# Ten units of the first block as seven products of block sums instead of eight block products

## The chip, the cores and the metric

The kernel runs on one core of a Trainium2 chip. The metric is the device time of one execution in microseconds. The engines named below are TensorE (PE: matmul; PEld: its weight loads), VectorE (DVE), ScalarE (ACT), GpSimd (POOL) and SyncE (SP, which here only starts DMAs). They run side by side and wait for each other by semaphores. Each executes its own instructions in their written order.

## What is computed

Two blocks follow each other on 512 tokens of 1024 channels; the change lies in the first. Its reference, cut to what matters:

```python
h = rmsnorm(x, norm_g[l])
proj = jnp.einsum('bsd,dn->bsn', h, w_in[l])            # 1024 -> 12 x 1024
a_u, a_v, a_z, b_p, b_z, c_h, c_b, c_c, c_z, gate_logits = jnp.split(proj, SPLIT_OFFSETS, axis=-1)
ya = spatial_gating(gelu(a_u), gelu(a_v), ...) * silu(a_z)
yb = multiscale_pool(b_p, ...) * silu(b_z)
yc = c_b * causal_depthwise_conv(c_c * c_h, conv_w[l], conv_b[l]) * silu(c_z)
gates = sigmoid(gate_logits.reshape(bsz, s, 3, 1024))   # g0, g1, g2
merged = gates[:, :, 0] * (ya @ w_branch_a) + gates[:, :, 1] * (yb @ w_branch_b) + gates[:, :, 2] * (yc @ w_branch_c)
x = x + merged @ w_out
```

Everything is float32. Each float32 matrix is used as two parts that TensorE takes: a high part (rounded) and a low part (the rest). A product is three matmuls: high x high, high x low, low x high.

## The kernel before

A section is one 1024 x 1024 weight matrix applied to all 512 tokens; it has two units of 512 output channels (c_h.0, c_h.1). The list `JOBS` (L70 and after) names all jobs in the order in which TensorE does them: ..., b_z, pool.0, pool.1, g1, c_h, w_b, c_c, g2, c_b, c_z, w_c, w_out, and so on. It also holds how often a job's semaphores are raised, from which `chunks_before`, `used_after`, `act_after` and `dve_after` work out every wait.

A unit has four chunks of 256 input channels x 512 outputs, 512 KB each. SP loads a chunk into one of four slots of `WR` (`RING` = 4) as soon as VectorE has made the low part of the chunk that was there before. ScalarE copies it to `WH` (high part, `split`, L999) once TensorE is through with the chunk that used the slot; VectorE writes `WL` = `WR` - `WH` (`split`, L1570); TensorE waits for that (`low_ready`) and does 24 matmuls per chunk: two groups of 128 input channels, four banks of 128 outputs, three high and low combinations, each over 512 token columns (`unit`, L2471). A unit is 96 such matmuls and fills the four banks of its parity; the next unit has the other four. The tokens' high and low parts are `HH` and `HL` (from `h`) or `YH` and `YL` (from a branch).

The banks are then emptied: the g units by ScalarE with a sigmoid into `G` and c_h by ScalarE into `CH` (`evac`, L1037); c_c and c_b by VectorE, multiplied as they leave the bank (L1850, L1871), with the three taps of the convolution in between (L1855, L1861); c_z by ScalarE with silu through `TMP`. `merge` (L1829, L1831) multiplies a branch's product by its gate and adds it to `M`.

Around pool.1, VectorE multiplies the pooled branch into `CH` (L1811, L1816), ScalarE makes its high parts `YH` and VectorE its low parts `YL` (`y_low`, L1607), and then the four chunks of g1.1 are split. GpSimd computes tables in the first 126 us has two copies and two small memsets up to 232 us, and nothing more until after c_z. The second copy of the input, `X`, is loaded behind the chunks of c_h.

## Time and profile before

| | |
|---|---|
| time, median of 3 runs | 1618.98 us (1618.83 to 1619.22) |
| span of the profiled execution | 1617.1 us |
| busy: TensorE, weight loads | 1606.0 us (99%), 1344.3 us (83%) |
| busy: VectorE, ScalarE, GpSimd | 952.0 us (59%), 667.2 us (41%), 204.3 us (13%) |
| instructions | 19917 |

The span is the time from the first to the last instruction of one execution that was profiled; the runs' time has some 2 us more around it. A busy share is an average over stages, so what a stage is bound by is read from its waits and from the chain that ended last, which follows from the last instruction back to what released each. Matmuls overlap at their ends: two starts in a row show the pace, a single duration doesn't.

### The profile page before, as it was taken

To read this page: it belongs to the slowest core of one execution; us is meant where nothing else is said; L and a number is where in the kernel's file an instruction comes from. 1 tells how busy PE (TensorE), PEld (TensorE's weight loads), DVE (VectorE), ACT (ScalarE), POOL (GpSimd) and SP (SyncE) were. 2 spreads that over 40 slices of the span, in tenths; PEclk is the share of its full clock that TensorE was granted. 3 is DMA by queue.
4 is the path that set the end of the run, shared out by engine and by line. 5 is a ranking of instruction groups with operands and counts; after the bars stand their busy time and mean duration, and the time that the engine had idled before them with its cause. 6 is when DMAs were issued, how large, how long until landed. Compare 5 with 4: busy or idle time off the path is not lost.

```text
span 1617.1 us, 19917 instructions
## 1 busy us (share of the span) xinstructions
PE 1606.0 (99%) x7833; PEld 1344.3 (83%) x7833; DVE 952.0 (59%) x1325; ACT 667.2 (41%) x936; POOL 204.3 (13%) x237
## 2 busy tenths in 40 slices
PE   9999999999999999999999999999999999999998
PEld 7888888888888888888898889887888888888887
DVE  5267274663235424456899999985473535455357
ACT  5333342253222223335455454558255425343254
...
GB/s 243 172 171 135 164 118 93 76 93 103 157 96 98 95 103 92 102 93 80 314 166 204 189 194 220 105 205 182 194 72 93 66 90 106 54 77 91 79 77 66
DMA packets 152395, 207.41 MB, mean 128 GB/s; under 512 B 52289, under 2 KB 75509, under 8 KB 151670
## 3 DMA queue, kind: packets, MB, share of 16 engines
...
HBM read 191.53 MB, written 14.68 MB: 128 GB/s over the span
## 4 chain that ended last, share of the span: by engine, by line
PE 97%; DVE 1%; ACT 1%; DMA 0%; issue 0%; DVEq 0%; SPq 0%; ACTq 0%
PE PS L2471 82%; PE PS L2449 3%; PE PS L2839 1%; PE PS L2548 1%; PE PS L2789 1%; PE PS L2691 1%; PE PS L2869 1%; PE PS L2658 1%; PE PS L2641 0%; PE PS L2845 0%; PE PS L2717 0%; PE PS L2626 0%; PE PS L2715 0%; PE PS L2716 0%; ACT XN L1006 0%; PE PS L2826 0%
## 5 line engine op out<-in xcount | busy, mean ns | idle before, releaser
L2471 PE MATMUL PS<-HH,WH 128*128 128x512 f32 x1216 | 474.7, 390 | 0.8 <-ACT G L1037 0.4
L2471 PE MATMUL PS<-HH,WL 128*128 128x512 f32 x1216 | 473.3, 389 | 0.0
L2471 PE MATMUL PS<-HL,WH 128*128 128x512 f32 x1216 | 473.2, 389 | 0.0
L999 ACT ACTIVATE WH<-WR 128x1024 fp32r<-128x1024 f32 x200 | 211.9, 1061 | 596.9 <-PE PS L2471 558.9
L1570 DVE TENSOR_TENSOR WL<-WR,WH 128x1024 fp32r<-128x1024 f32 x144 | 186.1, 1299 | 391.9 <-ACT WH L999 391.3
L2471 PEld LDWEIGHTS PS<-HH,WH 128*128 128x128 f32 x1216 | 228.3, 188 | 49.4 <-issue 2.1
L2471 PEld LDWEIGHTS PS<-HH,WL 128*128 128x128 f32 x1216 | 228.3, 188 | 47.8
L2471 PEld LDWEIGHTS PS<-HL,WH 128*128 128x128 f32 x1216 | 228.3, 188 | 47.0
L2022 DVE SCALAR_TENSOR_TENSOR TMP<-CP,PRM,TMP 128x512 f32<-128x512 f32 x232 | 155.0, 748 | 0.0
L2471 PE MATMUL PS<-WH,HH 128*128 128x512 f32 x320 | 126.8, 396 | 0.0
L2471 PE MATMUL PS<-WL,HH 128*128 128x512 f32 x320 | 125.1, 391 | 0.0
L2471 PE MATMUL PS<-WH,HL 128*128 128x512 f32 x320 | 125.1, 391 | 0.0
L2471 PE MATMUL PS<-YH,WH 128*128 128x512 f32 x320 | 124.6, 389 | 0.0
L2471 PE MATMUL PS<-YH,WL 128*128 128x512 f32 x320 | 124.5, 389 | 0.0
L2471 PE MATMUL PS<-YL,WH 128*128 128x512 f32 x320 | 124.5, 389 | 0.0
L1601 DVE TENSOR_TENSOR WL<-WR,WH 128x1024 fp32r<-128x1024 f32 x64 | 76.3, 1220 | 52.5 <-ACT WH L1025 52.5
L1025 ACT ACTIVATE WH<-WR 128x1024 fp32r<-128x1024 f32 x64 | 66.3, 1058 | 83.0 <-PE PS L2471 81.8
L2471 PEld LDWEIGHTS PS<-WH,HH 128*128 128x128 f32 x320 | 67.9, 212 | 13.1 <-issue 3.0
L2471 PEld LDWEIGHTS PS<-WH,HL 128*128 128x128 f32 x320 | 67.9, 212 | 10.5 <-issue 0.7
L2471 PEld LDWEIGHTS PS<-WL,HH 128*128 128x128 f32 x320 | 67.9, 212 | 10.1
L2471 PEld LDWEIGHTS PS<-YL,WH 128*128 128x128 f32 x320 | 60.1, 188 | 12.5
L2471 PEld LDWEIGHTS PS<-YH,WH 128*128 128x128 f32 x320 | 60.1, 188 | 12.5
...
## 6 DMA issues: line engine op xcount, KB each, us to landing
WR<-in_w_in_dram SPq DMA_DIRECT2D x96, 512.0 KB, 3.8
WR<-in_od_w_in_dram SPq DMA_DIRECT2D x32, 512.0 KB, 4.0
WR<-in_ev_w_in_dram SPq DMA_DIRECT2D x24, 512.0 KB, 4.6
WL<-in_ev_w_in_dram POOLq DMA_DIRECT2D x24, 512.0 KB, 7.6
WR<-in_ev_w_in_dram SPq DMA_DIRECT2D x32, 256.0 KB, 3.1
WR<-in_ev_w_out_dram SPq DMA_DIRECT2D x16, 512.0 KB, 5.3
WR<-in_od_w_in_dram SPq DMA_DIRECT2D x32, 256.0 KB, 3.4
WR<-in_od_w_out_dram SPq DMA_DIRECT2D x16, 512.0 KB, 3.8
```

The source lines that it names most:

```text
L999: act.activation(WH[:, n % RING, :, :], WR[:, n % RING, :, :], ACT.Copy).then_inc(w_hi, 1)
L1025: act.activation(WH[:, j % RING, :, :], WR[:, j % RING, :, :], ACT.Copy).then_inc(w_hi, 1)
L1570: dve.tensor_tensor(WL[:, s, :, :], WR[:, s, :, :], WH[:, s, :, :].bitcast(F32), ALU.subtract).then_inc(w_lo, SUM_TO - SUM_FROM + 1 if n = ...
L1601: dve.tensor_tensor(WL[:, s, :, :], WR[:, s, :, :], WH[:, s, :, :].bitcast(F32), ALU.subtract).then_inc(w_lo, 1)
L2022: o = dve.scalar_tensor_tensor(CP[:, kt, CPAD:] if last else TMP[:, s, :], CP[:, kt, k:k + SEQ], w, TMP[:, s, :], ALU.mult, ALU.add)
L2449: mm = pe.matmul(out_banks[m], tok(acts(kt)[ai], m), (WH, WL)[wi][:, q, kk, :], start=(kt == 0 and i == 0), stop=(kt == KT - 1 and i == 2))
L2471: mm = pe.matmul(out_banks[m], st, mv, start=(kt == 0 and i == 0), stop=(kt == 2 * per - 1 and i == 2))
L2548: mm = pe.matmul(bank("a_v.0", t), tile(H(2 * q + kk)[ai], t), (WH, WL)[wi][:, q, kk, :], start=(q == 0 and kk == 0 and i == 0), stop=(q = ...
L2658: mm = pe.matmul(bank(f"pool.{i}", m), (PWH, PWL)[wi][:, g, k, (kt % 2) * P:(kt % 2 + 1) * P], Y(2 * g + k)[ai], start=(k == 0 and j == 0) ...
L2691: mm = pe.matmul(bank(f"s5_z.{i}", m)[:, r * P:(r + 1) * P], WT[m // 2][:, pr, :], UT[:, pr, :], start=True, stop=True)
L2789: mm = pe.matmul(out_bank[:, cols], tile(acts(kt)[ai], t), (WH, WL)[wi][:, 2 * u + kt // 2, kt % 2, cols], start=(kt == 0 and i == 0), sto ...
L2839: mm = pe.matmul(A[m][:, s * P:SEQ], (V2, V2L)[wi][:, s, m * P:(m + 1) * P], scores, start=(s == 0 and i == 0), stop=(s == TT - 1 and i == ...
```

## The change

The ten units of c_h, c_c, g2, c_b and c_z become products of 2 x 2 blocks: halves of the tokens (256), of the input channels (512) and of the unit's outputs (256). Eight block products would be the same work as before; here seven products of sums of blocks are made, and their sums give the four output blocks.

- Each product is 24 matmuls of 256 columns (four groups of input channels, two of outputs, three high and low combinations). The seven operands of a unit are split like chunks, each of the same size as before (128 x 1024), in the four slots of `WH` and `WL`.
- SP loads the four weight blocks of a unit into places 0 to 3 of the `WR` region (rows of 1 KB instead of 2 KB). GpSimd adds blocks in place: W0 += W1, W1 += W2, W0 += W2, W3 += W0. The operands are, in order: block 0, sum 1, sum 2, sum 3, block 3, block 2, sum 4. A place is loaded again for the next unit when its last operand is split; place 0 when the fourth sum is made.
- The sums of token blocks are made once. When pool.1 is done, GpSimd does ten additions or subtractions of 128 x 1024 (from `HH` and `HL`); ScalarE and VectorE split the four results into high and low parts. The fourth replaces a block of `HH` and `HL`, once g1.1 is done.
- Products go to banks 0, 1, 3, 2 and then again 0, 1, 3, without clearing for the last three. ScalarE copies bank 0 out after product 0 and again after product 4. VectorE makes five combinations of a bank with a block already in SBUF; product 5 waits for the second, product 6 for the third, since they read the banks that these products go on with.
- In VectorE's queue these five stand between the low parts of the own and of the following unit. The side work (taps, products with c_b and c_z, low parts of Y) is dealt out between them as `others`, up to eight operations per unit, from c_c.1 on. It now reads SBUF only, since the combined units lie there. The sigmoid of g2 and the silu of c_z are done in place behind the combinations.
- The load of `X` moves behind c_z.1. Four semaphores of the tables become one.

The core of the diff:

```diff
-_section("c_h", a=4)
+_seven("c_h", (0, 2))
 _section("w_b", d=4)
-_section("c_c", d=4)
-_section("g2", a=4)
-_section("c_b", d=4)
-_section("c_z", a=4)
+_seven("c_c")
+_seven("g2")
+_seven("c_b")
+_seven("c_z")
...
+BLOCK_AT = ((0, 0), (0, 1), (1, 1), (1, 0))
+OPERAND_AT = (0, 0, 1, 0, 3, 2, 3)
+OPERAND_SUM = {1: 1, 2: 2, 3: 3, 6: 4}
...
+                for place in (1, 0, 2, 3) if again else range(4):
+                    if again and place == 0:
+                        sp.wait_ge(sums_made, sums_after(j - 1))
+                    elif again:
+                        sp.wait_ge(w_lo, chunks_before(before) + (0, 3, 6, 7)[place])
+                    else:
+                        sp.wait_ge(w_lo, n0 - RING + place + 1)
+                    i, half = BLOCK_AT[place]
+                    c0 = W_IN[name] + int(u) * NC + half * (NC // 2)
+                    sp.dma_start(WRS[:, place, :, :], w_in[4 * P * i:4 * P * (i + 1), c0:c0 + NC // 2]
+                                 .rearrange("(k p) n -> p k n", p=P)).then_inc(w_loaded[place], 16)
...
+            pool.wait_ge(side_done, side_after("pool.1"))
+            tt(S1R[:, :, :], h_part(HH, 1, 1), h_part(HH, 1, 0), ALU.subtract)
+            tt(STMP[:, :, :], h_part(HL, 1, 1), h_part(HL, 1, 0), ALU.subtract)
+            seq.wait()
+            pool.tensor_tensor(S1R[:, :, :], S1R[:, :, :], STMP[:, :, :], ALU.add).then_inc(sums_made, 1)
...
+            def add_block(to, other):
+                pool.tensor_tensor(WRS[:, to, :, :], WRS[:, to, :, :], WRS[:, other, :, :], ALU.add).then_inc(sums_made, 1)
+            for j, job in enumerate(SEVEN):
+                n0 = chunks_before(job)
+                pool.wait_ge(w_loaded[1], 16 * block_loads(job))
+                pool.wait_ge(w_lo, n0 + 1)
+                add_block(0, 1)
+                pool.wait_ge(w_loaded[2], 16 * block_loads(job))
+                add_block(1, 2)
+                pool.wait_ge(w_lo, n0 + 2)
+                pool.wait_ge(sums_made, sums_after(j, 1))
+                add_block(0, 2)
+                pool.wait_ge(w_lo, n0 + 5)
+                pool.wait_ge(sums_made, sums_after(j, 3))
+                add_block(3, 0)
...
+                act.wait_ge(weights_used, n0 + 1)
+                act.activation(block_of(to, 1, 1, kt0, skip), paired(job, 0), ACT.Copy).then_inc(banks_act, 1)
+                for i in range(4, 7):
+                    high(job, i)
+                if between:
+                    between()
+                next_high(following, 0)
+                act.wait_ge(weights_used, n0 + 5)
+                act.activation(block_of(to, 0, 0, kt0, skip), paired(job, 0), func).then_inc(banks_act, 1)
+                next_high(following, 1)
+                finish(1, 1, 3)
+                next_high(following, 2)
+                finish(0, 1, 4)
+                next_high(following, 3)
+                finish(1, 0, 5)
...
+            combination_hi(1, S1H[:, :, :], S1R[:, :, :])
+            combination_hi(2, S2H[:, :, :], S2R[:, :, :])
+            combination_hi(3, S4H[:, :, :], S4R[:, :, :])
+            for i in range(3):
+                high("c_h.0", i)
...
+                for i in range(3):
+                    low(job, 4 + i)
+                    others(paces[i])
+                dve.wait_ge(banks_act, act_after(job, 1))
+                dve.wait_ge(weights_used, n0 + 4)
+                dve.tensor_tensor(c21, c22, c, ALU.subtract).then_inc(banks_dve, 1)
+                dve.wait_ge(banks_dve, dve_after(job, 1))
+                dve.tensor_tensor(c22, c21, b, ALU.add).then_inc(banks_dve, 1)
+                next_low(following, 0)
+                dve.wait_ge(banks_dve, dve_after(job, 2))
+                dve.scalar_tensor_tensor(c22, c22, -1.0, d, ALU.mult, ALU.subtract).then_inc(banks_dve, 1)
+                others(paces[3])
+                next_low(following, 1)
+                dve.wait_ge(weights_used, n0 + 6)
+                dve.scalar_tensor_tensor(c12, c21, -1.0, b, ALU.mult, ALU.subtract).then_inc(banks_dve, 1)
+                others(paces[4])
+                next_low(following, 2)
+                dve.wait_ge(weights_used, n0 + 7)
+                dve.tensor_tensor(c21, c21, d, ALU.add).then_inc(banks_dve, 1)
+                others(paces[5])
+                next_low(following, 3)
...
+            combination_lo(1, S1L[:, :, :], S1R[:, :, :], S1H[:, :, :], 2)
+            combination_lo(2, S2L[:, :, :], S2R[:, :, :], S2H[:, :, :], 3)
+            combination_lo(3, S4L[:, :, :], S4R[:, :, :], S4H[:, :, :])
+            for i in range(3):
+                low("c_h.0", i)
+            combination_lo(4, corner(HL, 1, 0), S3R[:, :, :], corner(HH, 1, 0))
+            low("c_h.0", 3)
...
+            seven("c_c.0", U, "c_c.1")
+            taps0, taps1 = convolved(0), convolved(1)
+            seven("c_c.1", U, "g2.0", taps0)
+            seven("g2.0", G, "g2.1", taps0)
+            seven("g2.1", G, "c_b.0", taps1)
+            seven("c_b.0", CH, "c_b.1", taps1, skip=PPAD)
+            seven("c_b.1", CH, "c_z.0", weighed(0), skip=PPAD)
+            seven("c_z.0", CH, "c_z.1", weighed(1), skip=PPAD)
+            seven("c_z.1", CH, "w_c.0", gated_c(0), (2, 2, 0, 1, 1, 2), PPAD)
...
+            def seven(job):
+                n0 = chunks_before(job)
+                for i, (m, x) in enumerate(zip((0, 1, 3, 2, 0, 1, 3), blocks)):
+                    n = n0 + i
+                    low_ready(n)
+                    if i < 4:
+                        free_bank(job, m)
+                    elif i == 4:
+                        pe.wait_ge(banks_act, act_after(job, 1))
+                    else:
+                        pe.wait_ge(banks_dve, dve_after(job, i - 3))
+                    if job == SEVEN[0] and i in (1, 2):
+                        pe.wait_ge(parts_dve, (1, 4)[i - 1])
+                    for kt in range(4):
+                        for half in range(2):
+                            out_cols = slice(half * (SEQ // 2), (half + 1) * (SEQ // 2))
+                            for j, (wi, ai) in enumerate(halves):
+                                mm = pe.matmul(bank(job, m)[:, out_cols], (WHS, WLS)[wi][:, n % RING, kt, half * P:(half + 1) * P],
+                                               x[ai][:, kt, :], start=(i < 4 and kt == 0 and half == 0 and j == 0),
+                                               stop=(kt == 3 and half == 1 and j == 2), skip_group_check=True)
+                    mm.then_inc(weights_used, used_after(job) - n if i == 6 else 1)
```

## Rows read from the trace of the kernel before

**Rows 1.** The page: busy times, the chain's shares, a group of weight loads.

```profile
PE 1606.0 (99%) x7833; PEld 1344.3 (83%) x7833; DVE 952.0 (59%) x1325; ACT 667.2 (41%) x936; POOL 204.3 (13%) x237
...
PE 97%; DVE 1%; ACT 1%; DMA 0%; issue 0%; DVEq 0%; SPq 0%; ACTq 0%
...
L2471 PEld LDWEIGHTS PS<-HH,WH 128*128 128x128 f32 x1216 | 228.3, 188 | 49.4 <-issue 2.1
```

**Rows 2.** Waits, whole span: who waited for whom, us in total, times, longest.

```profile
ACT WH L999 <- PE PS L2471: 558.9, 155, 4.7
...
DVE WL L1570 <- ACT WH L999: 391.3, 106, 9.7
```

**Rows 3.** Timeline of TensorE, last output tile: start us, us, what, count.

```profile
1596.10 0.39 PE L2789 MATMUL PS<-WL,OH 128*128 128x512 f32 x1
...
1608.34 0.39 PE L2789 MATMUL PS<-WL,OH 128*128 128x512 f32 x1
1608.56 0.28 PE L2789 MATMUL PS<-WH,OH 128*128 128x256 f32 x1
...
1610.47 0.28 PE L2789 MATMUL PS<-WH,OL 128*128 128x256 f32 x1
```

**Rows 4.** Timeline of GpSimd, 89 to 126 us: start us, us, what, count.

```profile
89.69 1.31 POOL L794 TENSOR_TENSOR GRE<-PT 128x512 f32<-128x512 f32 x1
...
102.04 1.92 POOL L794 TENSOR_TENSOR PT<-GRE,LS 128x512 f32<-128x512 f32 x1
104.04 1.93 POOL L794 TENSOR_TENSOR PT<-GNI,LS 128x512 f32<-128x512 f32 x1
...
121.20 4.94 POOL L896 TENSOR_TENSOR TM<-TM,DT 128x2048 f32<-128x2048 f32 x1
```

**Rows 5.** Timeline of VectorE, the same stretch.

```profile
88.94 1.23 DVE L1674 BATCH_NORM_STATS2 BNS<-V 128x6 f32<-128x512 f32 x2
...
101.54 5.50 DVE L1570 TENSOR_TENSOR WL<-WR,WH 128x1024 fp32r<-128x1024 f32 x3 [9.74 <-ACT WH L999]
...
110.55 11.12 DVE L1682 TENSOR_SCALAR V<-V,BNA,STAT 128x1024 f32<-128x1024 f32 x4
121.59 6.77 DVE L1570 TENSOR_TENSOR WL<-WR,WH 128x1024 fp32r<-128x1024 f32 x2
```

**Rows 6.** Line 1570, the low parts: ns min/median/max, first and last start.

```profile
L1570 DVE TENSOR_TENSOR WL<-WR,WH x144: 1210/1226/5632, 10.4 to 1175.5; 128x1024 fp32r<-128x1024 f32 x144
```

**Rows 7.** Groups of VectorE by form: busy us, mean ns, idle before.

```profile
L1829 DVE TENSOR_TENSOR TMP<-PS,G 128x512 f32<-128x512 f32 x16 | 10.9, 683 | 0.0
L1861 DVE SCALAR_TENSOR_TENSOR U<-CH,PRM,U 128x512 f32<-128x512 f32 x16 | 10.8, 744 | 0.0
L1624 DVE TENSOR_TENSOR U<-U,TMP 128x512 f32<-128x512 f32 x16 | 10.3, 686 | 1.0 <-ACT TMP L1051 0.8
...
L1855 DVE TENSOR_SCALAR U<-CH,PRM 128x512 f32<-128x512 f32 x8 | 3.8, 539 | 0.0
```

**Rows 8.** Groups of ScalarE by form.

```profile
L999 ACT ACTIVATE WH<-WR 128x1024 fp32r<-128x1024 f32 x200 | 211.9, 1061 | 596.9 <-PE PS L2471 558.9 <-DMA WR<-in_w_in_dram 17.8 <-DMA WR<-in_ev_w_in_dram 16.8
...
L1037 ACT ACTIVATE CH<-PS 128x512 f32<-128x512 f32 x24 | 12.3, 598 | 0.0
```

**Rows 9.** DMA issues: count, KB each, median us to landing.

```profile
WR<-in_w_in_dram SPq DMA_DIRECT2D x96, 512.0 KB, 3.8
...
WR<-in_od_w_in_dram SPq DMA_DIRECT2D x32, 256.0 KB, 3.4
```

**Rows 10.** Timeline of VectorE during g1.

```profile
361.50 4.91 DVE L1607 TENSOR_TENSOR YL<-CH,YH 128x512 fp32r<-128x512 f32 x8
366.32 2.35 DVE L1570 TENSOR_TENSOR WL<-WR,WH 128x1024 fp32r<-128x1024 f32 x2
```

**Rows 11.** Windows: length, busy PE, PEld, DVE, ACT, POOL, clock, DMA share, GB/s.

```profile
485.50:660.00 174.50, 174.50 (x772) 144.53 (x771) 72.69 (x88) 43.39 (x50) 0.00 (x0) 1.00 0.32 98
1611.70:1617.00 5.30, 0.00 (x0) 0.00 (x0) 2.36 (x5) 1.03 (x4) 0.00 (x0) 0.70 0.26 100
```

More of the change, by code:

```diff
@@ L79, in _section, with _seven @@
         _add(f"{name}.{u}", chunks, 0, a, d)
+SEVEN = []
+def _seven(name, ends=(0, 0)):
+    for u in range(2):
+        SEVEN.append(f"{name}.{u}")
+        _add(f"{name}.{u}", 7 + ends[u], 0, 2, 5)
 _add("params", side=1, a=2)
@@ L169, with block_loads, sums_after, gate_acts @@
 PAIRED = {chunks_before(f"b_vg.{i}") + q for i in range(4) for q in range(4)}
+SEVEN_FROM = {chunks_before(name): used_after(name) for name in SEVEN}
+IN_SEVEN = {n for n0, n1 in SEVEN_FROM.items() for n in range(n0, n1)}
 def transfers(n, since=0):
-    return sum(2 if m in PAIRED else 1 for m in range(n % RING, n + 1, RING) if m >= since)
+    return (sum(2 if m in PAIRED else 1 for m in range(n % RING, n + 1, RING) if m >= since and m not in IN_SEVEN)
+            + sum(since <= n0 <= n for n0 in SEVEN_FROM))
+def block_loads(job):
+    whole = sum(n not in IN_SEVEN for n in range(chunks_before(job)))
+    return whole // RING + SEVEN.index(job) + 1
+BLOCK_AT = ((0, 0), (0, 1), (1, 1), (1, 0))
+OPERAND_AT = (0, 0, 1, 0, 3, 2, 3)
+OPERAND_SUM = {1: 1, 2: 2, 3: 3, 6: 4}
+COMBINED = 4
+def sums_after(j, k=4):
+    return COMBINED + 4 * j + k
+def gate_acts(section, u):
+    return COMBINED + 6 * ("g2", "c_z").index(section) + 3 * u + 3
+def taps_after(u):
+    return COMBINED + 4 * u + 4
+def weighed_after(u):
+    return COMBINED + KT + 4 * u + 4
 SUM_FROM, SUM_TO = chunks_before("a_in.0"), chunks_before("ev_b.0")
@@ L626, in _ @@
             section("g1", w_in, W_IN["g1"])
-            section("c_h", w_in, W_IN["c_h"])
-            sp.wait_ge(side_done, side_after("pool.1"))
-            sp.wait_ge(s5_out, 16 * S5_OUT)
+            for job in SEVEN[0:2]:
+                blocks(job)
+            sp.wait_ge(sums_made, sums_after(1))
+            section("w_b", a["w_branch_b"][0], 0)
+            for job in SEVEN[2:]:
+                blocks(job)
+            sp.wait_ge(sums_made, sums_after(len(SEVEN) - 1))
+            section("w_c", a["w_branch_c"][0], 0)
+            sp.wait_ge(weights_used, used_after("c_z.1"))
             sp.dma_start(X[:, :, :], x_d).then_inc(x_again, 16)
             sp.dma_start(FROW[:, :], a["final_g"].rearrange("(o n) -> o n", o=1).broadcast_to([P, D])).then_inc(frow_in, 16)
-            section("w_b", a["w_branch_b"][0], 0)
-            for name in ("c_c", "g2", "c_b", "c_z"):
-                section(name, w_in, W_IN[name])
-            section("w_c", a["w_branch_c"][0], 0)
             section("w_out", a["w_out"][0], 0)
@@ new lines, in _ @@
+            combination_hi(4, corner(HH, 1, 0), S3R[:, :, :])
+            high("c_h.0", 3)
+            evac("g1.1", [G[:, 4 + m, :] for m in range(4)], ACT.Sigmoid)
+            act.wait_ge(y_lo, 24)
+            seven("c_h.0", CH, "c_h.1", skip=PPAD)
+            seven("c_h.1", CH, "w_b.0", skip=PPAD)
+            split()
+            for i in range(4):
+                high("c_c.0", i)
+            act.wait_ge(parts_dve, 4)
+            seven("c_c.0", U, "c_c.1")
+            seven("c_c.1", U, "g2.0")
@@ L1840, in _, with convolved @@
             merge("w_b.0", 0)
-            split()
+            for i in range(4):
+                low("c_c.0", i)
             merge("w_b.1", 1)
-            for u in range(2):
-                split()
-                done(f"c_c.{u}")
-                dve.wait_ge(banks_act, act_after(f"c_h.{u}"))
+            def convolved(u):
+                dve.wait_ge(banks_act, act_after(f"c_c.{u}"))
+                dve.wait_ge(banks_dve, dve_after(f"c_c.{u}"))
+                at = [0] * 4
                 for m in range(4):
@@ L1863, in _ @@
[L1863 to L1877 removed]
+                        seq.wait(at[m])
@@ new lines, in _ @@
+            seven("c_c.0", U, "c_c.1")
+            taps0, taps1 = convolved(0), convolved(1)
[6 more added lines that the diff above has]
+            seven("c_z.1", CH, "w_c.0", gated_c(0), (2, 2, 0, 1, 1, 2), PPAD)
+            for _ in gated_c(1):
+                pass
```

217 lines of the change are left out of this document (153 added, 64 removed).

## The prediction

> **What bounds the kernel now.** I read the page's busy shares and its chain of waits first: TensorE is busy for 1606.0 of 1617.1 us and is 97% of the chain that ended last [rows 1]. Then who waits for whom: ScalarE, which makes the high parts of the weights, waits 559 us for TensorE, and VectorE, which makes the low parts, 391 us for ScalarE [rows 2]. So in the stretch to be changed the matmul stream sets the time and the rest has slack: in the eight units from c_c to c_z (485.5 to 660 us) VectorE is busy for 72.7 of 174.5 us, ScalarE for 43.4, GpSimd not at all [rows 11]. The change takes work from TensorE and gives all three others more, so I ask which of them takes over.
>
> **The products.** A matmul over 512 columns starts every 0.2267 us (54 of them from 1596.10 to 1608.34), one over 256 columns every 0.1194 us (16 steps in 1.91 us) [rows 3]. A unit is now 96 x 0.2267 = 21.76 us, afterwards 7 x 24 x 0.1194 = 20.06 us, a product 2.87 us. Ten units: -17.0 us, as long as nothing makes TensorE wait. This is all that the change can give.
>
> **Prices of the other work.** High part 1.06 us, evacuation 0.60 us on ScalarE [rows 8]. Low part 1.22 us on VectorE [rows 6]. Each of the five combinations of a unit reads one bank and one SBUF block: 0.68 us, like TMP<-PS,G; the two in scalar_tensor_tensor form 0.74, like the taps. Side work: multiplication 0.69, tap 0.74, first tap 0.54 us [rows 7]. Consecutive VectorE operations overlap by 0.08 us. A GpSimd addition with two full inputs took 1.31 us at 512 elements (89.69 us) and 4.94 us at 2048, of which some 0.45 was waiting: it was sent off at 121.20, and VectorE's operation before ended at 110.55 + 11.12 = 121.67 us [rows 4, 5]: 0.23 us plus 2.08 ns per element, so 2.36 us at 1024. A 512 KB load lands after 3.8 us; the new block loads have rows of 1 KB, as the 256 KB loads that took 3.4 us have [rows 9]; between 3.8 and 2 x 3.4 us I take 4.5, near the row of equal size.
>
> **GpSimd and VectorE exclude each other.** From 101.54 us three low parts took 5.50 us instead of 3.5, and two GpSimd operations beside them 1.92 and 1.93 us, more than the 1.31 of the longest of their size that met no such operation: one runs, then the other [rows 4, 5]. A low part that met the 4.94 us addition took 5.63 us, against a median of 1.23 [rows 6]. The two batch-norm operations at 88.94 us, with one SBUF input each, slowed nothing and were not slowed [rows 4, 5]. The step in the alternation is 2.00 us (102.04 to 104.04); a low part of 1.22 and a GpSimd operation of some 1.06 us are 2.28, so some 0.28 us per pair does overlap; I carry about half of it at each change of hands, and 0.07 us between GpSimd's own operations. The Trainium skill says the same (SBUF — State Buffer, Who interferes with whom): a VectorE instruction with two SBUF inputs contends with a GpSimd instruction that reads SBUF, and the second to issue fully blocks. It speaks against this change; by that rule, the trace agrees. For the five combinations (a bank and one SBUF block) no row shows the case; the batch-norm row is nearest, so I let them pass. If they block too, the sum grows by some 10 us.
>
> **Demand of a unit.** GpSimd 4 x 2.36 = 9.4 us, low parts 7 x 1.22 = 8.5 us, side work 8 operations, 5.4 us: 23.4 us that exclude each other, less some 1 us of overlap, against 20.06 us of TensorE (and against 21.76 us before). Without side work it is 18.0 us, but then dependence counts: low part 4, fourth sum, refetch of block 0, high and low part of the next unit's operand 0, its first sum.
>
> **One unit carried forward.** I took the queues in their written order, each operation starting at the latest of its inputs, its engine and the other engine's exclusion. In g2.1, counted from its first matmul: low part 4 ends at 9.8 us; GpSimd's fourth sum waits for one side operation and runs from 10.25 to 12.6; VectorE's next operation waits for that and ends at 13.15; low part 5 at 14.3, two side operations 15.5, low part 6 at 16.65, one more 17.1, then the first two combinations, 17.7 and 18.4. Product 5 waits for the second one (its bank): it starts at 18.5 instead of 14.4. Block 0 has landed at 17.15, and the chain repeats. So TensorE waits 4.1 us in this unit. Likewise: c_h.0 0; c_c.0 2.6; c_c.1 3.0; g2.0 3.5; g2.1 4.1; c_b.0 4.1; c_b.1 3.8; c_z.0 1.9; c_z.1 3.0. In c_h.1 VectorE's third combination is queued behind w_b.0's first low part, whose slot comes free only with the end of product 5; product 6 waits for that combination: 1.06 + 1.22 + 0.74 = 3.0 us, with 0.8 before it, 3.8. All ten: 29.8 us.
>
> **The token sums, during g1.** GpSimd starts ten additions of 1024 elements when pool.1 ends at 354.9 us. VectorE then still has four multiplications of CH (up to 361.5 us), eight low parts of Y (from there, 4.91 us long) and then the low part for g1.1 (366.32 us) [rows 10]. TensorE needs that one when g1.0 is through, at 354.9 + 21.8 = 376.6 us: 9 us of slack now. Alternating with 2.36 us additions, each short operation costs a step of 2.75 us; ten steps are 27.5 us, the remaining low parts of Y and the weight's end at 385.3 us. TensorE waits 8.7 us. The block that is overwritten last (fourth sum, then its high and low part) is ready in time.
>
> **The clock.** In the 5.3 us after the last matmul the mean granted clock was 0.70 [rows 11]: between the levels 2.4 and 1.2 GHz that is 3.2 us at the lower. A wait of 8.7 us will lower it too. What it costs after the restart no row shows: 0 to 1.6 us (3.2 us at half speed); I take 1.5, since this wait is longer than the idle of that row. For the 2 to 4 us waits within units I take 0, at most 1.6 us each.
>
> **At no cost**: moving the load of X behind c_z.1 (8.7 us long, needed over 60 us later), the joined semaphores, the gates' activation in place (three operations of 0.6 us on ScalarE, idle for three quarters of this stretch), more DMA (four blocks of 512 KB in 20.06 us, 105 GB/s where 98 were [rows 11]). If ScalarE's cover were gone its operations would delay the next evacuation by as much.
>
> **The sum.** -17.0 + 8.7 + 29.8 + 1.5 = +23.0 us. Profiled span 1617.1 -> 1640.1; the median of the runs is 1618.98, 1.9 us above the span, so 1642.0. Carried again with other prices: additions of 2.1 us give 11 us less, 2.5 us 6 more; loads of 4.0 us 2 less, 5.5 us 7 more; no overlap between VectorE's operations 9 more.
>
> **Rivals.**
> - *The exclusion is absent or hidden* (other side). The carried schedule without it waits 3.1 us at the end of c_h.1, 5.4 us elsewhere (the loop through the refetch), and none in g1: -17.0 + 8.5 = -8.5, 1610.5 us. It decides if additions block low parts for under some 1.8 us each. For: the 0.28 us that overlap. Against: [rows 4 to 6]. Chance 0.13.
> - *Half of it*: additions of 1.8 us, a third above the 1.31 us of half the size: 1619 us, no change. Chance 0.07.
> - *Heavier*: block loads of 5.5 us or combinations that block too, and the clock down in some units: 1655 us. Chance 0.12.
> - *It doesn't do what it says*: a weight load per matmul lasts 0.188 us [rows 1]; were it not overlapped at 256 columns, a unit would be 168 x 0.188 = 31.6 us, 1717 us. The rows at 256 columns have such loads too and start every 0.119 us [rows 3]. Chance 0.02.
>
> **The numbers.** The forecast case has 0.66, with its own range 1630 to 1655. A measurement of this kernel tells 0.2% (3.2 us) from no change. Faster 0.15, within 0.2% 0.06, slower 0.79. Range: 1620 to 1658, leaving out most of the faster rival, the last one and the ends.
>
> **What would show it.** TensorE's waits put down to VectorE's second combination; GpSimd additions with a mean well over 2.4 us and low parts in these units well over 1.23; a wait of some 9 us before g1.1; units of 22 to 24 us. It is wrong if units come at 20 us, if the additions take under 2 us, or if the low part for g1.1 is ready by 376 us.

## The result, and the profile after

| | before | after |
|---|---|---|
| time, median (lowest to highest) | 1618.90 us (1618.74 to 1619.22) | 1649.47 us (1647.24 to 1649.56) |
| span of the profiled execution | 1617.1 us | 1647.7 us |
| mean granted clock of TensorE | 1.00 | 0.988 |

The changed kernel takes 1.0185 times as long, 95% interval 1.0172 to 1.0197: 30.6 us slower, where 23.0 were forecast, inside the range.

The page of the changed kernel: busy times, the chain's shares, two groups of section 5 (one of GpSimd's block sums, one of VectorE's low parts) and the block loads of section 6.

```profile
PE 1603.7 (97%) x8553; PEld 1375.4 (83%) x8553; DVE 1090.2 (66%) x1409; ACT 706.2 (43%) x978; POOL 333.4 (20%) x287
...
PE 81%; DVE 10%; DMA 3%; ACT 3%; POOL 1%; issue 1%; SPq 0%; DVEq 0%; ACTq 0%; POOLq 0%
...
L1026 POOL TENSOR_TENSOR WRS<-WRS 128x1024 f32<-128x1024 f32 x40 | 101.3, 2542 | 191.8 <-DVE WLS L1768 191.8
L1768 DVE TENSOR_TENSOR WLS<-WRS,WHS 128x1024 fp32r<-128x1024 f32 x70 | 106.0, 1521 | 51.2 <-ACT WHS L1147 51.1
...
WRS<-in_w_in_dram SPq DMA_DIRECT2D x40, 512.0 KB, 4.4
```

TensorE was 97% of the chain that ended last [rows 1]; now 81%, and VectorE has 10%. TensorE's busy time fell by only 2.3 us although an eighth of the work of ten units is gone, so part of its matmuls ran slower. A low part lasts 1.52 us on average (1.23 before [rows 6]), a block addition 2.54.

Who waited for whom, TensorE's rows (us in total, times, longest). L2962 are the seven products, L2749 the old kind of unit; L1795 is VectorE's second combination, L1798 its third, L1759 a low part of the old kind.

```profile
PE PS L2962 <- DVE CH L1795: 9.6, 5, 2.9
PE PS L2749 <- DVE WL L1759: 9.3, 1, 9.3
PE PS L2962 <- DVE G L1795: 5.9, 2, 3.7
PE PS L2962 <- DVE U L1795: 4.3, 2, 2.3
PE PS L2962 <- DVE CH L1798: 3.2, 1, 3.2
```

That is 19.8 us for the second combination in nine units, 3.2 for the third in one, 9.3 for the low part of g1.1: 32.3 us.

Groups of VectorE by form (busy us, mean ns): low parts of Y, then first and later taps.

```profile
L1843 DVE TENSOR_TENSOR YL<-CH,YH 128x512 fp32r<-128x512 f32 x8 | 18.1, 2326 | 0.0
L2106 DVE TENSOR_SCALAR U<-CH,PRM 128x512 f32<-128x512 f32 x8 | 11.2, 1406 | 0.0
L2113 DVE SCALAR_TENSOR_TENSOR U<-CH,PRM,U 128x512 f32<-128x512 f32 x16 | 23.3, 1475 | 0.0
```

The eight low parts of Y took 4.91 us together before [rows 10], the taps 0.54 and 0.74 us each [rows 7].

Windows of the changed kernel: length, busy PE, PEld, DVE, ACT, POOL, granted clock, DMA share, GB/s. The first is g1. Then c_h.0, c_h.1, c_c.0, c_c.1, g2.0, g2.1, c_b.0, c_b.1, c_z.0 and c_z.1; the last is all that follows.

```profile
354.80:410.40 55.60, 46.29 (x192) 37.71 (x191) 41.86 (x27) 16.54 (x20) 34.56 (x13) 0.91 0.15 47
410.50:430.30 19.80, 19.80 (x169) 19.72 (x169) 11.36 (x9) 10.13 (x13) 5.90 (x3) 1.00 0.27 82
430.35:457.00 26.65, 21.95 (x171) 21.41 (x170) 14.18 (x12) 7.11 (x8) 6.91 (x3) 0.94 0.30 100
...
500.50:524.00 23.50, 21.50 (x170) 21.31 (x169) 14.01 (x17) 7.34 (x8) 7.81 (x3) 0.93 0.22 69
524.00:546.20 22.20, 19.87 (x170) 19.70 (x169) 21.33 (x19) 8.17 (x9) 9.92 (x5) 1.00 0.31 96
546.20:572.30 26.10, 22.44 (x171) 22.26 (x170) 25.49 (x22) 9.75 (x11) 11.26 (x6) 0.87 0.27 81
572.30:596.00 23.70, 21.47 (x170) 21.29 (x169) 22.49 (x21) 9.96 (x12) 9.73 (x5) 0.93 0.29 89
596.00:620.20 24.20, 21.56 (x170) 21.39 (x169) 23.05 (x20) 9.31 (x11) 10.35 (x4) 0.93 0.29 88
620.20:644.20 24.00, 21.56 (x170) 21.39 (x169) 20.45 (x20) 8.40 (x10) 10.17 (x5) 0.93 0.30 88
644.20:664.30 20.10, 19.92 (x170) 19.75 (x169) 17.00 (x16) 9.22 (x10) 9.44 (x4) 1.00 0.35 106
664.30:688.80 24.50, 21.56 (x171) 21.39 (x170) 21.99 (x21) 13.81 (x18) 5.42 (x3) 0.93 0.40 127
688.80:1647.70 958.90, 951.23 (x4673) 800.95 (x4671) 649.21 (x966) 454.26 (x653) 101.25 (x106) 1.00 0.51 133
```

The same two outer stretches of the kernel before, g1 and all after c_z:

```profile
354.80:398.35 43.55, 43.55 (x193) 36.06 (x193) 19.79 (x25) 13.91 (x18) 0.00 (x0) 1.00 0.27 81
660.00:1617.10 957.10, 950.46 (x4671) 800.83 (x4669) 647.06 (x963) 455.39 (x656) 101.25 (x106) 1.00 0.50 130
```

This table separates two costs. Length minus busy PE is time in which TensorE stood. Busy PE above that of an undisturbed unit is matmuls at the lower clock. A unit that never stands takes 19.80 us (c_h.0); c_c.1 stands for 2.33 us and is busy for 19.87. c_c.0 stands for 2.00 us, but is busy for 21.50, at a mean clock of 0.93: 1.6 us of work more from the same 168 matmuls. The balance, in us of the span:

| | forecast | measured | from |
|---|---|---|---|
| ten units, undisturbed | -17.0 | -19.6 | 10 x (19.80 - 21.76 [rows 3]) |
| waits within units | +29.8 | +23.0 | waits, four rows |
| wait of g1.1 | +8.7 | +9.3 | waits, second row |
| half-speed matmuls in g1 | +1.5 | +2.7 | 46.29 - 43.55 |
| half-speed matmuls in units | 0 | +13.0 | busy PE of the ten, 211.6, less 10 x 19.86 (mean of the three at clock 1.00) |
| after c_z | 0 | +1.8 | 958.90 - 957.10 |
| sum | +23.0 | +30.2 | the span moved by 30.6 |

An undisturbed unit is taken at 19.80 us in the first row and at 19.86 in the fifth; with 19.80 in both the fifth is 13.6, so this balance is good to about half a microsecond.

### The profile page after: what moved, and what is told of

Same layout as the page of the kernel before. It is cut to its first block, busy times and chain, and to the rows that moved or that the text cites. A ratio compares the mean times of both kernels' runs of the same rounds, so it can differ in the third digit from the quotient of the medians.

```text
span 1647.7 us, 21495 instructions
## 1 busy us (share of the span) xinstructions
PE 1603.7 (97%) x8553; PEld 1375.4 (83%) x8553; DVE 1090.2 (66%) x1409; ACT 706.2 (43%) x978; POOL 333.4 (20%) x287
## 4 chain that ended last, share of the span: by engine, by line
PE 81%; DVE 10%; DMA 3%; ACT 3%; POOL 1%; issue 1%; SPq 0%; DVEq 0%; ACTq 0%; POOLq 0%
PE PS L2749 64%; DVE WLS L1768 4%; PE PS L2727 3%; PE PS L2962 2%; POOL WRS L1026 1%; PE PS L3143 1%; DMA WR<-in_ev_w_in_dram 1%; PE PS L2826 1%; PE PS L3093 1%; ACT WHS L1147 1%; PE PS L2995 1%; DVE U L2113 1%; PE PS L3173 1%; PE PS L2936 1%; DMA WL<-in_ev_w_out_dram 1%
## 5 line engine op out<-in xcount | busy, mean ns | idle before, releaser
L2749 PE MATMUL PS<-HH,WH 128*128 128x512 f32 x896 | 351.6, 392 | 10.1 <-DVE WL L1759 9.3
L2749 PE MATMUL PS<-HL,WH 128*128 128x512 f32 x896 | 349.8, 390 | 0.0
L2749 PE MATMUL PS<-HH,WL 128*128 128x512 f32 x896 | 349.8, 390 | 0.0
L1759 DVE TENSOR_TENSOR WL<-WR,WH 128x1024 fp32r<-128x1024 f32 x104 | 137.8, 1336 | 226.6 <-ACT WH L1133 226.2
L2749 PEld LDWEIGHTS PS<-HH,WH 128*128 128x128 f32 x896 | 168.9, 188 | 47.3 <-DVE WL L1759 9.7
L2749 PEld LDWEIGHTS PS<-HH,WL 128*128 128x128 f32 x896 | 168.9, 188 | 35.5
L2749 PEld LDWEIGHTS PS<-HL,WH 128*128 128x128 f32 x896 | 168.9, 189 | 34.6
L1026 POOL TENSOR_TENSOR WRS<-WRS 128x1024 f32<-128x1024 f32 x40 | 101.3, 2542 | 191.8 <-DVE WLS L1768 191.8
L1768 DVE TENSOR_TENSOR WLS<-WRS,WHS 128x1024 fp32r<-128x1024 f32 x70 | 106.0, 1521 | 51.2 <-ACT WHS L1147 51.1
L1147 ACT ACTIVATE WHS<-WRS 128x1024 fp32r<-128x1024 f32 x70 | 73.4, 1059 | 153.0 <-POOL WRS L1026 97.1
L2749 PE MATMUL PS<-WH,HH 128*128 128x512 f32 x320 | 127.0, 397 | 1.1 <-DMA WL<-in_ev_w_out_dram 0.6
L2749 PE MATMUL PS<-WL,HH 128*128 128x512 f32 x320 | 125.1, 391 | 0.0
L2749 PE MATMUL PS<-WH,HL 128*128 128x512 f32 x320 | 125.1, 391 | 0.0
L2749 PE MATMUL PS<-YH,WH 128*128 128x512 f32 x320 | 124.6, 389 | 0.0
L2749 PE MATMUL PS<-YH,WL 128*128 128x512 f32 x320 | 124.5, 389 | 0.0
L2749 PE MATMUL PS<-YL,WH 128*128 128x512 f32 x320 | 124.5, 389 | 0.0
L2962 PE MATMUL PS<-HH,WHS 128*128 128x256 f32 x320 | 91.7, 287 | 3.3 <-DVE CH L1798 3.2
L2962 PE MATMUL PS<-HH,WLS 128*128 128x256 f32 x320 | 91.2, 285 | 0.0
```

The lines of the kernel that those rows point to most:

```text
L1026: pool.tensor_tensor(WRS[:, to, :, :], WRS[:, to, :, :], WRS[:, other, :, :], ALU.add).then_inc(sums_made, 1)
L1147: act.activation(WHS[:, n % RING, :, :], WRS[:, OPERAND_AT[i], :, :], ACT.Copy).then_inc(w_hi, ends)
L1759: dve.tensor_tensor(WL[:, s, :, :], WR[:, s, :, :], WH[:, s, :, :].bitcast(F32), ALU.subtract).then_inc(w_lo, SUM_TO - SUM_FROM + 1 if n = ...
L1768: dve.tensor_tensor(WLS[:, n % RING, :, :], WRS[:, OPERAND_AT[i], :, :], WHS[:, n % RING, :, :].bitcast(F32), ALU.subtract).then_inc(w_lo, ...
L2749: mm = pe.matmul(out_banks[m], st, mv, start=(kt == 0 and i == 0), stop=(kt == 2 * per - 1 and i == 2))
L2962: mm = pe.matmul(bank(job, m)[:, out_cols], (WHS, WLS)[wi][:, n % RING, kt, half * P:(half + 1) * P], x[ai][:, kt, :], start=(i < 4 and kt ...
```

## The experiments

The theory after the result: (1) GpSimd's additions and VectorE's operations with two SBUF inputs exclude each other; (2) the order of VectorE's queue places two waits, that of g1.1 and that in c_h.1; (3) waits above some 2 us are followed by matmuls at half speed, which is where the forecast was short; the time is then TensorE's. The rivals: the loop through the block sums costs the same whatever GpSimd excludes; the half-speed matmuls run beside work that sets the time anyway, so a full clock gives nothing back. The first five runs change one thing each in the changed kernel.

### The block sums away

```diff
-pool.tensor_tensor(WRS[:, to, :, :], WRS[:, to, :, :], WRS[:, other, :, :], ALU.add).then_inc(sums_made, 1)
+pool.memset(WRS[:, to, 0:1, 0:1], 0.0).then_inc(sums_made, 1)
```

The units then multiply blocks that were not summed, so this kernel leaves out part of the computation.

> The changed kernel with each of the 40 block additions on GpSimd replaced by a memset of one element in the same place and with the same waits, so the units multiply unsummed blocks (part of the computation is left out). The ten token sums stay. Theory A (the additions and VectorE's two-input operations exclude each other, and that makes TensorE wait within the units): the waits for the second combination vanish except at the end of c_h.1, units take about 19.8 us, the time falls from 1649.5 to about 1619 us (-19.6 for the products, +12 in g1, +6 in c_h.1). Rival B (the clock or the matmuls themselves are what is slow): units stay at 22 to 24 us and the time above 1640.

Measured: 1613.83 us (1612.32 to 1616.50), ratio 0.9969 (0.9957 to 0.9980). Its waits of TensorE, the low parts, and the window of c_h.1:

```profile
PE PS L2749 <- DVE WL L1759: 9.3, 1, 9.3
PE PS L2962 <- DVE CH L1798: 3.2, 1, 3.2
...
L1768 DVE TENSOR_TENSOR WLS<-WRS,WHS 128x1024 fp32r<-128x1024 f32 x70 | 85.6, 1223 | 58.7 <-ACT WHS L1147 58.2
...
429.40:452.50 23.10, 19.95 (x170) 19.78 (x169) 8.79 (x9) 6.28 (x7) 0.10 (x1) 1.00 0.36 115
```

All waits for the second combination are gone with the additions, and so is every half-speed matmul in units: the block sums bring 35.6 of the change's time. The wait of g1.1 and the one of 3.2 us in c_h.1 stay, so these two are not the block sums' doing. The run came 5 us under its expectation, which had 6 us for c_h.1. The window shows 3.15 us of standing in c_h.1, and no half-speed matmul after it.

### Memsets as long as the additions

The same place, written but not read: per sum two memsets of 128 x 1024 and one of 128 x 512, 2.45 us together. The sums themselves are left out again.

```diff
-pool.tensor_tensor(WRS[:, to, :, :], WRS[:, to, :, :], WRS[:, other, :, :], ALU.add).then_inc(sums_made, 1)
+for _ in range(2):
+    seq.inc(pool.memset(WRS[:, to, :, :], 0.0))
+    seq.wait()
+pool.memset(WRS[:, to, 0:2, :], 0.0).then_inc(sums_made, 1)
```

> The changed kernel with each block addition replaced by memsets of the same place that last about as long together (2.4 to 2.5 us) but read nothing from SBUF, so the chain of waits and its latency stays and only the reading beside VectorE goes (part of the computation is left out). Theory A (exclusion): low parts go back to 1.22 us, the waits within c_c.1 to c_z.1 fall to 1 to 2 us each, the time to about 1629. Rival C (no exclusion is needed: the latency of addition, refetch and split alone closes a loop longer than a unit): waits and time as in the changed kernel, 1645 to 1650.

Measured: 1627.28 us, ratio 1.0051 (1.0028 to 1.0073). Low parts, GpSimd's memsets, and first taps, and TensorE's waits for the third and the second combination in CH (4.3 us more are in the rows of G and U):

```profile
L1771 DVE TENSOR_TENSOR WLS<-WRS,WHS 128x1024 fp32r<-128x1024 f32 x70 | 85.5, 1224 | 77.5 <-ACT WHS L1150 77.4
L1027 POOL MEMSET WRS<- 128x1024 f32 x80 | 77.0, 963 | 175.9 <-DVE WLS L1771 173.6
L2109 DVE TENSOR_SCALAR U<-CH,PRM 128x512 f32<-128x512 f32 x8 | 5.4, 681 | 0.0
...
PE PS L2965 <- DVE CH L1801: 4.4, 4, 3.2
PE PS L2965 <- DVE CH L1798: 1.9, 2, 1.4
```

GpSimd is nearly as long busy and every dependence is the same, but the low parts keep their 1.22 us. So it is GpSimd's additions, which read SBUF, that stop the low parts, not its being busy and not its writes. First taps are another case: they read one SBUF tensor, the additions held them too (0.54 us before, 1.41 in the changed kernel), and even beside memsets half of them take 0.80 to 0.84 us. The block sums' 35.6 us split into 13.4 that come with their duration in the loop (1613.8 to 1627.3) and 22.2 that come with the exclusion (1627.3 to 1649.5). Both parts have half-speed matmuls in them. In c_h.1 the wait is 3.15 us in this run and in the one before, but here the unit is busy for 22.5 us and there for 19.95, so the split is uncertain by some 2.5 us. The first rival falls all the same: dependence alone is the smaller part.

### The low parts of g1.1 earlier

```diff
-y_low(2, lambda kt: CH[:, kt, PPAD:], range(8))
-split()
+for q in range(4):
+    split(1)
+    y_low(2, lambda kt: CH[:, kt, PPAD:], (2 * q, 2 * q + 1))
```

> The changed kernel with one order altered: VectorE makes the low parts of g1.1's four chunks between pairs of the eight low parts of Y, not behind all eight. Theory A: the wait of 9.3 us before g1.1 goes, and with it the lower clock behind it (2.9 us), so 12 us less: 1637.5. If the token sums delay something else in g1 just as much (their own high and low parts, needed by c_h.0), less than 5 us are won.

Measured: 1639.19 us, ratio 1.0125. The wait of 9.3 us is gone and c_h.0 begins at 398.0 us. Its waits now:

```profile
PE PS L2963 <- DVE CH L1795: 12.0, 6, 3.0
PE PS L2963 <- DVE G L1795: 6.0, 2, 4.0
```

A sixth unit with CH has joined: c_h.0, whose operands are now late themselves, since the ten token sums end when they did. 9.3 us of waiting and 2.7 of half speed were removed, 10.3 us gained.

### The third combination before the next low part

```diff
-next_low(following, 0)
 dve.wait_ge(banks_dve, dve_after(job, 2))
 dve.scalar_tensor_tensor(c22, c22, -1.0, d, ALU.mult, ALU.subtract).then_inc(banks_dve, 1)
+next_low(following, 0)
```

> The changed kernel with VectorE's third combination in every unit placed ahead of the following unit's first low part. The 3.3 us wait of product 6 in c_h.1 goes, and the half-speed matmuls behind it (some 3 us): 1649.5 - 6 = 1643.5. If the low part that is now 0.7 us later is on the loop through the sums, the other eight units each lose up to 0.7 us and it comes out at 1645 to 1649.

Measured: 1648.01 us, ratio 1.0180. The row of the third combination is gone. Those of the second:

```profile
PE PS L2962 <- DVE CH L1795: 12.5, 5, 3.5
PE PS L2962 <- DVE G L1795: 5.3, 2, 3.0
PE PS L2962 <- DVE U L1795: 4.9, 2, 2.9
```

22.7 us in place of 19.8 + 3.2. c_h.1 is 4.7 us shorter (21.95 against 26.65), and the eight units from c_c.0 are together 3.4 us longer (191.7 against 188.3). The operand of the following unit comes later by one combination in each unit, its first block sum with it; that this is what gives back c_h.1's gain is the alternative of the expectation, and it fits. The whole gain is 1.5 us, and both executions (1647.72 and 1648.30 us) lie within the spread of the changed kernel's (1647.24 to 1649.56), so it is not clear of noise. The queue behind w_b.0 (prediction: 3.0 us) is real, but here removing it moves the time by little or nothing.

### Filling the wait

Before product 5, fourteen transposes of the identity into a bank that is free.

```diff
+if i == 5:
+    before = NAMES[NAMES.index(job) - 1]
+    pe.wait_ge(banks_act, act_after(before))
+    pe.wait_ge(banks_dve, dve_after(before))
+    for _ in range(14):
+        pe.transpose(bank(before, 0)[:, 0:P], ident[:, :], ident[:, :])
 pe.wait_ge(banks_dve, dve_after(job, i - 3))
```

> The changed kernel with 14 transposes of the identity (some 1.4 us of TensorE's own work, into a bank of the other parity that is long empty) ahead of product 5 in each of the ten units, where TensorE waits anyway. Theory D (the half-speed matmuls behind the longer waits come from the idle time before them, and cost about 1.5 us in each of six units): gaps shrink from 2.2 to 3.8 us to 0.8 to 2.4 us, product 5 takes 2.8 us again in most of them, and the time falls by some 9 us, less 1.4 in c_h.0 and 1 in c_z.0 that had no such wait: 1643. Rival E (the slow product 5 has another cause, such as contention for its operands): it stays slow and the time rises by 1 to 3 us: 1651 to 1653.

Measured: 1648.97 us, ratio 1.0184. Windows of c_h.0, then of g2.1, c_b.0 and c_b.1, and of c_z.1:

```profile
410.50:431.90 21.40, 21.40 (x184) 21.36 (x183) 12.70 (x10) 10.20 (x14) 7.15 (x3) 1.00 0.25 79
...
572.40:595.60 23.20, 21.64 (x185) 21.41 (x185) 21.99 (x21) 9.45 (x12) 9.79 (x4) 1.00 0.30 91
595.60:621.30 25.70, 23.05 (x185) 22.81 (x184) 24.54 (x21) 10.31 (x12) 10.79 (x5) 0.93 0.27 82
621.30:643.70 22.40, 21.43 (x184) 21.19 (x183) 18.81 (x19) 7.43 (x9) 9.64 (x4) 1.00 0.32 95
...
665.50:688.40 22.90, 21.51 (x185) 21.27 (x184) 21.86 (x21) 13.83 (x18) 5.47 (x3) 1.00 0.36 123
```

The time is that of the changed kernel. The fillers cost 1.60 us (21.40 - 19.80 in c_h.0, which never stood). Seven of the ten units now have a clock of 1.00, where three had. Over the ten, from the windows: standing 14.3 us, and busy PE 220.0 us, which is 21.4 above ten units at 19.86 (16 of it fillers, 5.4 half speed); 35.7 us in place of 23.0 + 13.0.

Unit by unit the equal time is a sum of gains and losses. c_b.1 and c_z.1 have their clock back and are each 1.6 us shorter than in the changed kernel (22.40 against 24.00, 22.90 against 24.50): there the clock's time came back in full. g2.1 has it back too and is only 0.5 us shorter (23.20 against 23.70). The three units that had a full clock already, c_h.0, c_c.1 and c_z.0, are 1.6, 1.0 and 1.7 us longer, and c_b.0, whose clock stays at 0.93, is 1.5 us longer and stands for 2.65 us with fillers and all. So this run does not decide the second rival. Half speed cost 7.6 us less in all, and the three units that had a full clock already took 4.3 us more with their fillers. That VectorE and GpSimd set the length of the others fits g2.1, but is argued. What part of the 13.0 us a full clock without fillers would give back stays open.

### All sums on VectorE

VectorE makes the token sums between the low parts of g1.1 and Y, and each block sum behind the low part that frees its place: the first and second behind low part 0, the third behind 1, the fourth behind 4. GpSimd does nothing in this stretch.

```diff
+def low_sums(job, i):
+    low(job, i)
+    for k in {0: (1, 2), 1: (3,), 4: (4,)}.get(i, ()):
+        block_sum(job, k)
...
-    low(job, 4 + i)
+    low_sums(job, 4 + i)
```

> The seven products as in the changed kernel, but all sums, of token blocks and of weight blocks, are made by VectorE (1.22 us each) in its own queue, the token sums spread between the low parts of g1.1 and of Y. GpSimd does nothing in this stretch. Theory A (GpSimd's additions cost VectorE 2.36 us each of blocked time and more where it waits in turn): VectorE's load per unit with side work is 11 x 1.14 + 3.1 + 5 = 20.6 us, close to a unit's 19.8, the waits before product 5 fall to 0 to 1.6 us, only c_h.1 keeps its 3.1 us (and 1.6 of clock): 1618.9 - 8.8 = 1610. Rival F (VectorE is the bound by its amount of work, whoever adds): with 4 more operations per unit on it, units take 23 us and more, 1640 or above.

Measured: 1616.22 us, ratio 0.9982 (0.9972 to 0.9992). Beside the run with the other order in g1 (1639.19 us), one engine does what two did, and 23.0 us go. It missed its expectation by 6 us. TensorE waits 11.8 us in these units, all for the third combination, 3.2 of it in c_h.1: this combination now stands behind the next unit's low part and two block sums. The next run takes it out of that place. The window of c_h.1:

```profile
417.60:442.20 24.60, 21.45 (x171) 21.28 (x171) 11.55 (x13) 6.28 (x7) 0.00 (x0) 0.93 0.34 108
```

TensorE stands here for 3.15 us, in the same unit and ahead of the same product as in the kernel without block sums. There the unit was busy for 19.95 us at a clock of 1.00, here for 21.45 at 0.93. The length of a wait alone does not decide what it costs.

### All sums on VectorE, and the third combination first

Both edits together.

> As the kernel before it, with the third combination ahead of the following unit's first low part. The wait at the end of c_h.1 goes: 1610 - 4.5 = 1606. If the order costs the other units more than it gives, 1610 or above.

Measured: 1604.71 us (1604.18 to 1605.74), ratio 0.9910 (0.9893 to 0.9926), 14.3 us faster than before the change. Windows of c_h.0 with c_h.1, and of g2.1:

```profile
398.60:438.00 39.40, 39.40 (x338) 39.36 (x338) 26.75 (x26) 17.59 (x21) 0.00 (x0) 1.00 0.30 97
...
541.80:563.20 21.40, 19.96 (x171) 19.79 (x170) 20.82 (x25) 9.86 (x12) 0.00 (x0) 1.00 0.32 99
```

The edit that moved the time by 1.5 us beside the exclusion, within the noise, gives 11.5 here: 6.7 of waits (11.8 to 5.1) and the rest half-speed matmuls, since the clock is now 1.00 throughout. Two units come in 39.4 us. In g2.1 TensorE stands for 1.44 of 21.40 us and VectorE is busy for 20.82, so VectorE is likely the bound there now; a run below tests it.

### Idle TensorE, in ten lengths

On the kernel of the last section, product 5 also waits for a chain of tiny memsets on the idle GpSimd, 8 to 26 of them, another number in each unit.

```diff
+for j, job in enumerate(SEVEN):
+    pool.wait_ge(weights_used, chunks_before(job) + 5)
+    for k in range(IDLES[j]):
+        ... pool.memset(IDLE[:, :], 0.0), the last one .then_inc(cpads, 1)
...
+if i == 5:
+    pe.wait_ge(cpads, SEVEN.index(job) + 1)
```

> On top of the kernel with all sums on VectorE and the third combination first (1604.7 us, units of 19.7 to 21.5 us, clock 1.00 throughout). In each of the ten units product 5 also waits for a chain of small GpSimd memsets that starts with the end of product 4; GpSimd does nothing else there. The chains have 8, 14, 20, 11, 17, 26, 12, 15, 18 and 22 memsets; at an estimated 0.2 us each that is 1.6, 2.8, 4.0, 2.2, 3.4, 5.2, 2.4, 3.0, 3.6 and 4.4 us of idle TensorE, 32.6 us in all in place of 5.7: 1631.6 us if idling costs only itself. Theory (length decides): every wait above some 2.1 us is followed by half-speed matmuls that cost 1.6 us more, so nine of the ten units pay it and the one of 1.6 us doesn't: 1646 us. Rival (length alone doesn't decide): of the units with 2.2 to 3.6 us of idle some pay and some don't, in no order of length, while the longest pay up to 2.4 us: 1638 to 1643 us.

Measured: 1648.32 us (one execution, span 1646.5). TensorE's wait for the chains, and the windows of c_h.0, c_h.1, c_c.0, c_c.1, g2.0 and g2.1:

```profile
PE PS L2986 <- POOL IDLE L1014: 31.3, 10, 5.1
...
397.80:419.30 21.50, 19.90 (x169) 19.71 (x168) 16.91 (x16) 11.29 (x14) 0.99 (x8) 1.00 0.24 77
419.30:443.50 24.20, 21.51 (x170) 21.33 (x169) 10.01 (x10) 6.28 (x7) 1.74 (x14) 0.93 0.29 88
487.10:512.30 25.20, 21.41 (x170) 21.24 (x169) 21.02 (x23) 8.40 (x9) 2.49 (x20) 0.93 0.21 64
512.30:536.00 23.70, 21.55 (x171) 21.38 (x170) 20.16 (x23) 8.51 (x9) 1.36 (x11) 0.93 0.29 90
536.00:561.95 25.95, 22.71 (x170) 22.54 (x170) 21.39 (x24) 9.55 (x11) 2.11 (x17) 0.87 0.27 81
561.95:589.50 27.55, 22.47 (x170) 22.30 (x169) 20.73 (x24) 10.07 (x12) 3.43 (x26) 0.88 0.25 77
```

Standing (length minus busy) against busy: 1.60 us, 19.90; 2.15, 21.55; 2.69, 21.51; 3.24, 22.71; 3.79, 21.41; 5.08, 22.47. The other four stand for 2.3 to 4.2 us and are busy for 21.4 to 22.2. Every unit that stood for 2.15 us or more paid, by 1.5 to 2.8 us; the one at 1.60 paid nothing. Busy time of the ten is 216.2 us, 17.2 above ten at 19.90. With 31.3 us of standing in place of 5.1 (the waits before product 5 on its base) that makes 43.4; the span moved by 42.5 (from 1604.0). Here TensorE sets the time, and the clock costs in full. The theory's 1646 us is near, and in this one execution no unit of 2.15 us or more went free, where the rival had some pay and some not. But length does not order the costs either (3.24 us cost 2.8, 3.79 us 1.5), the changed kernel's c_c.1 stood for 2.33 us and paid nothing, and the same 3.15 us in c_h.1 cost nothing without block sums and 1.5 us with all sums on VectorE. What lets these through is open.

### What bounds the better version

Two more kernels on the base of the run before, all sums on VectorE and the third combination first. In the first the eight products c_c x c_h and the eight first taps are one column wide, so the convolution's input is left out:

```diff
-dve.tensor_tensor(CH[:, kt, PPAD:], U[:, kt, :], CH[:, kt, PPAD:], ALU.mult)
+dve.tensor_tensor(CH[:, kt, PPAD:PPAD + 1], U[:, kt, 0:1], CH[:, kt, PPAD:PPAD + 1], ALU.mult)
```

> On top of the kernel with all sums on VectorE and the third combination first (1604.7 us, which has 5.7 us of waits before product 5 in g2.0 to c_b.1). The eight multiplications of c_c with c_h and the eight first taps are cut to one column each, so the convolution's input is not computed. Theory (VectorE is the bound in those units, with 7 low parts, 4 sums, 5 combinations and 8 side operations for 19.8 us of products): 0.69 + 0.54 us less for each pair, waits of g2.0 and g2.1 go, those of c_b.0 and c_b.1 stay at 1.0 and 1.5 us: 1601.5 us. Rival (the loop through the load of block 0 is the bound): waits as they are, 1604.7 us.

Measured: 1601.11 us, ratio 0.9890 (0.9872 to 0.9907). The waits in g2 (2.3 us) went. Those in c_b.0 and c_b.1 fell from 2.8 to 1.5 us, where 2.5 were expected to stay. With less work for VectorE the waits shrink, which the rival, the loop through the load of block 0, did not allow: VectorE's load is the bound.

In the second only the dealing of the side operations changes:

```diff
-def seven(job, to, following, work=iter(()), paces=(2, 2, 1, 1, 1, 1), skip=0):
+def seven(job, to, following, work=iter(()), paces=(1, 1, 1, 1, 2, 2), skip=0):
...
-seven("c_b.1", CH, "c_z.0", weighed(0), skip=PPAD)
+seven("c_b.1", CH, "c_z.0", weighed(0), (1, 1, 0, 1, 1, 0), PPAD)
```

> On top of the kernel with all sums on VectorE and the third combination first (1604.7 us). The side operations are dealt out later in a unit: (1, 1, 1, 1, 2, 2) instead of (2, 2, 1, 1, 1, 1), and (1, 1, 0, 1, 1, 0) in c_b.1, so fewer stand ahead of the two combinations that product 5 waits for. Theory (VectorE's order ahead of the combinations): waits of 0.1, 1.6, 1.1, 1.6 and 0.2 us in g2.0, g2.1, c_b.0, c_b.1 and c_z.1, 4.6 in place of 5.7 to 6.6: 1603 us. Rival (VectorE's total in these units is the bound, whatever the order): 1604.7 us.

Measured: 1602.81 us (1602.23 to 1604.35), ratio 0.9899 (0.9881 to 0.9916): 16.2 us faster than before the change, the fastest kernel of the study that computes the whole. The 1.9 us to the version above lie where they were expected, but the two intervals overlap, so this last step is likely, not shown.

## Why the prediction was right, and where it was off

- **What bounds the kernel, and who takes over**: right. TensorE's share of the chain fell to 81%, and its waits are put down to VectorE's second combination in nine of ten units.
- **The products**, -17.0: measured -19.6. A unit is 19.80 us, not 168 x 0.1194 = 20.06. The term took the pace from 16 steps in one place; over a whole unit it is 0.1179 (19.80 / 168). In c_h.0 the products with `HH` and `HL` go at 0.119 us a matmul and those with the token sums at 0.114; why the latter are faster is open. The fourth rival, loads one after another, would give units of 31.6 us and falls. Weight loads are busy for 19.72 of the 19.80 us, but each lasts 0.19 us and one starts every 0.12, so in these rows they overlap one another, and the figure does not say how near they are to being the bound.
- **Exclusion**: right, and its sign decided the result. Memsets of the same length leave the low parts at 1.22 us, additions make them 1.52 and the later taps twice as long. The five combinations, which were let pass, did pass: the second took 0.69 us in all ten units. First taps, with one SBUF input, were held up to 2.31 us, which the prediction's account of two inputs does not cover. A step in g1 was forecast at 2.75 us. Here are GpSimd's first and last token sum, and VectorE's matching operations:

```profile
354.85 2.63 POOL L890 TENSOR_TENSOR S1R<-HH 128x1024 f32<-128x1024 f32 x1 [123.60 <-PE PS L2936]
...
380.22 2.68 POOL L1023 TENSOR_TENSOR S3R<-S3R,STMP 128x1024 f32<-128x1024 f32 x1
```

```profile
366.58 18.07 DVE L1843 TENSOR_TENSOR YL<-CH,YH 128x512 fp32r<-128x512 f32 x8
384.58 4.62 DVE L1759 TENSOR_TENSOR WL<-WR,WH 128x1024 fp32r<-128x1024 f32 x4
```

  Nine steps from 354.85 to 380.22 are 2.82 us each. The four low parts of g1.1 begin at 384.58, so the first ends near 385.8, where 385.3 was forecast, and the wait is 9.3 instead of 8.7. The Trainium skill (SBUF — State Buffer, Who interferes with whom) speaks of a GpSimd instruction that reads SBUF; by that rule memsets should pass and additions block, and the low parts agree: 1224 ns in the run with memsets, 1521 in the changed kernel with additions.
- **Prices**: loads of blocks 4.4 us (4.5 taken), additions 2.54 on average, contention included, against an estimated 2.36 alone.
- **The waits within units**, +29.8: measured +23.0. From the windows: c_h.0 0 (0), c_h.1 4.7 (3.8), c_c.0 2.0 (2.6), c_c.1 2.3 (3.0), g2.0 3.7 (3.5), g2.1 2.2 (4.1), c_b.0 2.6 (4.1), c_b.1 2.4 (3.8), c_z.0 0.2 (1.9), c_z.1 2.9 (3.0). The early ones hold; from g2.1 to c_z.0 the forecast is too high by 1.4 to 1.9 us. In three of these four the half-speed matmuls stretched the unit by some 1.6 us, time in which VectorE and GpSimd went on, which may have shortened the waits. The run with fillers shows such an exchange in g2.1, but not in c_b.1, so this is argued, not shown.
- **The clock**, +1.5: measured +2.7 in g1 and +13.0 in units. This is the mis-sized term. "For the 2 to 4 us waits within units I take 0, at most 1.6 us each": seven units paid 1.6 to 2.6 us each, two of them (c_h.1 and g2.0) more than that upper end. The one row at hand, a mean of 0.70 in 5.3 us of standing [rows 11], did not exclude that, and taking the lower end of 0 to 1.6 us for eight waits at once was the wrong choice. As a pair with the waits it was 29.8 forecast against 36.0 measured: waits 6.8 us too high and clock 13.0 too low. That the sum came as near as it did is in this part luck.
- **At no cost**: the stretch after c_z is 1.8 us longer (1.0 of standing, 0.8 of busy PE). Which of the edits that were costed at nothing does that is open.
- **Rivals**: the exclusion is there, so the first two fell. The time without it was given as 1610.5 us. The nearest run is the one with memsets, 1627.3 us, in which the wait of g1.1 and its half-speed matmuls (12.0 us) remain: some 1615 without them, an estimate. The third, with "the clock down in some units", at 1655 and a chance of 0.12, had the right mechanism in its last clause, and too small a chance for that; its other conditions did not come, the block loads took 4.4 us and the combinations passed.
